# Dilated attention in steps of four units: scores, values and transposes of two pairs at every fourth step

## What is computed

```python
DIL_PAIRS = ((128, 1), (512, 4), (2048, 16))      # window, dilation

def dilated_attention(q, k, v):                   # per block of 128 queries
    ...
    for gi in range(g):                           # three groups
        sc = einsum('bqhd,bqjhd->bhqj', q_blk[:, :, gi], k_sel) * scale
        sc = where(valid, sc, NEG_INF)
        m = max(sc); e = exp(sc - m); z = sum(e)
        o = einsum('bhqj,bqjhd->bqhd', e / z, v_sel)
        outs.append(o); lses.append(m + log(z))
    wgt = softmax(stack(lses))
    out = sum(wgt * stack(outs))
```

## Time and profile before

| | |
|---|---|
| median of 3 runs | 1209.13 us (1208.7 to 1209.37) |
| the profiled execution's own time | 1208.3 us |
| its span | 1206.5 us |
| PE busy in it | 1194.9 us, 99% |
| DVE busy | 840.1 us, 70% |
| ACT busy | 648.6 us, 54% |
| POOL busy | 219.7 us, 18% |
| granted TensorE clock, mean | 0.999 |

### The profile page before, as it was taken

The page is one execution under the profiler, slowest core; times in us unless marked ns, Lnnn a source line. Parts: engine busy times, 40 slices in busy tenths (PEclk is TensorE's granted clock), DMA queues, the critical chain, the costliest instruction groups (busy, mean ns, idle before and its releaser), DMA issues.

```text
span 1206.5 us, 18986 instructions
## 1 busy us (share of the span) xinstructions
PE 1194.9 (99%) x7681; PEld 1047.4 (87%) x7681; DVE 840.1 (70%) x1207; ACT 648.6 (54%) x887; POOL 219.7 (18%) x160
## 2 busy tenths in 40 slices
PE   9999999999999999999999999999999999999998
PEld 9988898888898888889888888898878899888886
DVE  7878768754467856886979754487875576676863
ACT  5575465543455556455555534456576545555452
POOL 2500010000011211331310000010010795545100
PEclk9999999999999999999999999999999999999999
DMA  9723456555548665664355565654544455556551
GB/s 254 250 87 124 140 175 187 197 181 203 179 147 272 199 203 160 186 207 156 114 183 186 177 207 176 209 174 156 179 171 140 171 183 184 178 179 196 184 190 55
DMA packets 162071, 214.08 MB, mean 177 GB/s; under 512 B 5260, under 2 KB 117199, under 8 KB 161983
## 3 DMA queue, kind: packets, MB, share of 16 engines
q1 hardware_dynamic: 161182, 211.41, 54.3%
q10 hardware_dynamic: 608, 0.99, 0.3%
q0 software_dynamic: 192, 0.46, 0.2%
HBM read 205.50 MB, written 1.05 MB: 171 GB/s over the span
## 4 chain that ended last, share of the span: by engine, by line
PE 92%; DVE 3%; ACT 2%; issue 1%; DMA 1%; SPq 0%; DVEq 0%; ACTq 0%
PE ps L541 45%; PE ps L556 20%; PE ps L561 11%; PE ps L641 4%; PE ps L742 3%; PE ps L779 2%; PE ps L750 2%; PE ps L583 2%; DVE wlo L1618 1%; ACT whi L1156 1%; PE ps L607 1%; DVE XT L1756 1%; DMA raw<-in_od_w_in_dram 1%; PE ps L867 1%; PE ps L1031 0%
## 5 line engine op out<-in xcount | busy, mean ns | idle before, releaser
L1618 DVE TENSOR_TENSOR wlo<-raw,whi 128x2048 fp32r<-128x2048 f32 (+1 forms) x167 | 383.8, 2300 | 143.3 <-ACT whi L1156 143.0
L1156 ACT ACTIVATE whi<-raw 128x2048 fp32r<-128x2048 f32 x188 | 357.8, 1906 | 170.3 <-PE ps L541 131.4
L556 PE MATMUL ps<-XHL,whi 128*128 128x512 f32 x1152 | 287.8, 394 | 0.0
L556 PEld LDWEIGHTS ps<-XHL,whi 128*128 128x128 f32 x1152 | 207.8, 189 | 38.1
L561 PEld LDWEIGHTS ps<-XHL,wlo 128*128 128x128 f32 x1152 | 154.8, 190 | 11.6 <-DVE wlo L1618 1.6
L561 PE MATMUL ps<-XHL,wlo 128*128 128x256 f32 x1152 | 158.5, 282 | 0.3 <-DVE wlo L1618 0.3
L541 PE MATMUL ps<-whi,XHL 128*128 128x512 f32 (+1 forms) x576 | 145.2, 345 | 0.0
L2360 POOL TENSOR_TENSOR wlo<-raw,whi 128x512 fp32r<-128x512 f32 x88 | 119.3, 1388 | 141.4 <-ACT whi L1156 141.1
L541 PE MATMUL ps<-whi,HL 128*128 128x512 f32 (+1 forms) x416 | 144.8, 373 | 0.0
L541 PE MATMUL ps<-whi,HH 128*128 128x512 f32 x384 | 143.3, 390 | 0.0
L541 PE MATMUL ps<-wlo,HH 128*128 128x512 f32 x368 | 139.4, 389 | 0.0
(11 more groups left out here) (273 smaller groups left out, 1738.9 us busy)
## 6 DMA issues: line engine op xcount, KB each, us to landing
raw<-in_mlp_w_dram SPq DMA_DIRECT2D x64, 1024.0 KB, 5.3
raw<-in_od_w_in_dram SPq DMA_DIRECT2D x36, 1024.0 KB, 5.3
raw<-in_w_in_dram SPq DMA_DIRECT2D x24, 1024.0 KB, 5.1
raw<-in_w_ffn_gate_dram SPq DMA_DIRECT2D x12, 1024.0 KB, 5.2
raw<-in_w_ffn_up_dram SPq DMA_DIRECT2D x12, 1024.0 KB, 5.2
raw<-in_w_ffn_down_dram SPq DMA_DIRECT2D x12, 1024.0 KB, 5.0
TB<-TA SPq DMA_DIRECT2D x96, 64.0 KB, 2.0
raw<-in_w_branch_dram SPq DMA_DIRECT2D x6, 1024.0 KB, 5.0
```

What stands on the lines that cost most here:

```text
L556: pe.matmul(b[m][:, :], w[m][c][0], XHL[:, c, :], start=c == 0, stop=False)
L1156: act.activation(whi_of(n), raw_of(n), ACT.Copy, scale=1.0).then_inc(*tell(s_whi, ("whi", n)))
L1618: dve.tensor_tensor(wlo_of(n), raw_of(n), f32(whi_of(n)), ALU.subtract).then_inc(*tell(s_wlo, ("wlo", n)))
```

## The change

The first 24 units go four at a time. At every fourth step PE has the scores of four units, then the values of two pairs, then the transposes of four units; the three steps between have only their slabs. DVE takes the four maxima at that step and two softmaxes at each of the two steps behind it; ACT takes the four exponentials. The two pairs' values share a bank, and their outputs become one operation of 256 columns on ACT and one on DVE. SN and PT (3 x 512 columns) are cut into four buffers of 384 for these units, the statistics get a fourth row. The last eight units go as before, with the values of pairs 10 and 11 together at step 26. Cut to its core:

```diff
+FOURS = 24
+
+def dilated_scores(s):
+    if s < FOURS:
+        return range(s, s + 4) if s % 4 == 0 else ()
+    return (s, s + 1) if s < 32 and s % 2 == 0 else ()
+
+def dilated_begun(s):
+    if s < FOURS:
+        return dilated_scores(s)
+    return (s,) if s < 32 else ()
+
+def dilated_scaled(s):
+    if s <= FOURS:
+        return {1: (s - 1, s), 2: (s, s + 1)}.get(s % 4, ())
+    return (s - 1,) if s < 33 else ()
+
+def dilated_turns(s):
+    if s <= FOURS:
+        return range(s - 4, s) if s and s % 4 == 0 else ()
+    return (s - 2,) if FOURS + 2 <= s < 34 else ()
+
+def dilated_values(s):
+    if 8 <= s <= FOURS and s % 4 == 0 or s == FOURS + 2:
+        g = (s - 8) // 2 if s <= FOURS else FOURS // 2 - 2
+        return (g, g + 1)
+    return ((s - 4) // 2,) if FOURS + 4 <= s < 35 and s % 2 == 0 else ()
+
+def before(u):
+    first, k = (EVEN, 3) if u < ODD else (ODD, 4) if u < LAST else (LAST, 3)
+    return u - k if u - k >= first else first - 1
...
+        def unit_of(t, u):
+            if kind_of(u)[0] != DIL:
+                return t[:, u % 3, :]
+            return t[:, :, :].rearrange("p a n -> p (a n)")[:, 384 * (u % 4):384 * (u % 4) + 384]
...
-            def values(g):
-                b = bank(("value", g))
+            def values(*gs):
+                b = bank(("value", gs[0]))
...
+            def attend_dilated(s):                                    # PE
+                for u in dilated_scores(s)[::2]:
+                    scores(group_of(ODD + u))
+                gs = [ODD // 2 + g for g in dilated_values(s)]
+                if gs:
+                    values(*gs)
+                for u in dilated_turns(s):
+                    transposes(ODD + u)
...
-                attend(ODD, 32, s)
+                attend_dilated(s)
...
-                if u >= 3:
-                    once.wait_ge(*at(("turned", u - 3)))
+                if before(u) >= 0:
+                    once.wait_ge(*at(("turned", before(u))))
...
+            def attend_dilated(s):                                    # ACT
+                gs = [ODD // 2 + g for g in dilated_values(s)]
+                if len(gs) == 2:
+                    outputs(*gs)
+                for u in dilated_turns(s) if s <= FOURS else ():
+                    if act_turns(ODD + u):
+                        probs(ODD + u)
+                for u in dilated_begun(s):
+                    exponentials(ODD + u)
+                for u in dilated_turns(s) if s > FOURS else ():
+                    if act_turns(ODD + u):
+                        probs(ODD + u)
+                if len(gs) == 1:
+                    outputs(*gs)
...
+            def attend_dilated(s, beside):                            # DVE
+                for u in dilated_begun(s):
+                    maxima(ODD + u)
+                for u in dilated_scaled(s):
+                    softmax(ODD + u)
+                for u in dilated_turns(s):
+                    if not act_turns(ODD + u):
+                        probs(ODD + u)
+                beside()
+                if dilated_values(s):
+                    outputs(*(ODD // 2 + g for g in dilated_values(s)))
...
-                attend(ODD, 32, s, lambda: added_pieces(s - 1))
+                attend_dilated(s, lambda: added_pieces(s - 1))
```

More of the change, by code:

```diff
@@ L766, in value_parts @@
                 return [(v[:, kt, w * n:w * n + w], (kt * S, kt * S + S), (0, S), kt == 0, kt == 1) for kt in range(2)]
[L768 to L780 removed]
+            def values(*gs):
+                b = bank(("value", gs[0]))
+                for g in gs:
+                    for u in members(g):
+                        once.wait_ge(*at(("probs", u)))
+                        for event in values_ready(u):
+                            once.wait_ge(*at(event))
+                    parts = {u: value_parts(u) for u in members(g)}
+                    for k in range(len(parts[members(g)[0]])):
+                        for u in members(g):
+                            v, (lo, hi), (a, z), start, stop = parts[u][k]
+                            p0, n, _, _ = place_of(u)
+                            m = pe.matmul(b[p0:p0 + n, a:z], v, unit_of(PT, u)[:, lo:hi], start=start, stop=stop)
+                    m.then_inc(*tell(s_value, ("valued", g)))
+            def attend_dilated(s):
[6 more added lines that the diff above has]
+                    transposes(ODD + u)
             def attend(first, n, s):
@@ L1227, in probs, with outputs @@
                 once.wait_ge(*at(("turned", u)))
-                if u >= 3:
-                    once.wait_ge(*at(("valued", group_of(u - 3))))
-                act.activation(PT[:, u % 3, 0:w], ps[bank_of.get(("turn", u), 0)][:, 0:w], ACT.Copy, scale=1.0).then_inc(
+                if before(u) >= 0:
+                    once.wait_ge(*at(("valued", group_of(before(u)))))
+                act.activation(unit_of(PT, u)[:, 0:w], ps[bank_of.get(("turn", u), 0)][:, 0:w], ACT.Copy, scale=1.0).then_inc(
                     *tell(s_act_out, ("probs", u), ("taken", "turn", u)))
-            def outputs(g):
-                _, _, c, (t0, t1) = place_of(members(g)[0])
-                h, v = OH[:, c, t0:t1], ps[bank_of.get(("value", g), 0)][:, 0:t1 - t0]
-                if g < 4:
-                    h, v = h.rearrange("p (r c) -> p r c", c=64), turned(v)
-                once.wait_ge(*at(("valued", g)))
-                act.activation(h, v, ACT.Copy, scale=1.0).then_inc(*tell(s_xhi, ("ohi", g)))
+            def outputs(*gs):
+                _, _, c, (t0, _) = place_of(members(gs[0])[0])
+                _, _, _, (_, t1) = place_of(members(gs[-1])[0])
+                h, v = OH[:, c, t0:t1], ps[bank_of.get(("value", gs[0]), 0)][:, t0:t1]
+                if gs[0] < 4:
+                    h, v = h.rearrange("p (r c) -> p r c", c=64), turned(v)
+                once.wait_ge(*at(("valued", gs[-1])))
+                act.activation(h, v, ACT.Copy, scale=1.0).then_inc(*tell(s_xhi, *[("ohi", g) for g in gs]))
+            def attend_dilated(s):
[12 more added lines that the diff above has]
+                    outputs(*gs)
             def attend(first, n, s):
@@ L1678, in maxima @@
                 kind, _ = kind_of(u)
-                b = ps[bank_of.get(("score", u), 0)]
+                b, st = ps[bank_of.get(("score", u), 0)], stat_of(u)
                 once.wait_ge(*at(("scored", u)))
-                if u >= 3:
-                    once.wait_ge(*at(("turned", u - 3)))
-                    once.wait_ge(*at(("soft", u - 3)))
+                if before(u) >= 0:
+                    once.wait_ge(*at(("turned", before(u))))
+                    once.wait_ge(*at(("soft", before(u))))
                 if kind in (NA, DIL, MOBA):
@@ L1729, in attend @@
                     softmax(u)
-                if not paired and 0 <= s - 2 < n and not act_turns(first + s - 2):
-                    probs(first + s - 2)
                 if beside is not None:
```

53 lines of the change are left out of this document (29 added, 24 removed).

## The result

The changed kernel takes 1211.61 us, the median of 14 runs (1210.41 to 1213.15), against 1208.80 for the kernel before on the same chip (14 runs): ratio 1.0022, 95% interval 1.0015 to 1.0029. It is slower by 2.8 us, where 0.4 faster was forecast; the range held the time. The profiled execution took 1211.98 us. In the changed kernel scores are line 796, values 836, transposes 804, pieces and value slabs 595, the other slabs 610 and 615, maxima 1770, the additions of pieces 1849.

What follows compares the result with a forecast made beforehand. PE was taken to bound the kernel, with DVE as close after step 24. Terms -3.2 + 4 x 0.4 + 0.4 + 2.2 - 1.2 = -0.2, taken as -0.4, gave 1208.7 us; range 1204.9 to 1212.2.

Steps and rivals of the forecast that it cites:

- merging: PE's scores, values, transposes and returns to slabs: fewer switches of kind save 0.53 us per four units, 3.2 us in all.
- ninth bank, steps 4 to 20: Merged steps need nine banks of eight, so PE waits for DVE's maxima: 0.4 us at each of five steps.
- step 24, the waits: Fourth transposes and next piece wait for banks until DVE's additions, queued behind unit 24's maxima: 2.2 us, between 1.3 and 2.4.
- probs in the tail: With PE later against DVE and ACT, its three waits for ACT's probs after step 24 go: 1.2 us back.
- Rival (b): DVE, held by POOL's sines, reaches blocks late; 0.8 us late at five blocks adds 4.0 us: 1212.7 us, chance 0.16.
- Rival (c): PE pays the switch of kind per bank, so the 3.2 us saving fails: 1211.9 us, chance 0.05.
- rival (a): Banks are read in time and never hold PE: 1204.7 us; chance 0.24 including a half-way case.
- A loss in low halves or loads would refute my account of what is covered: Sign against the claim that DVE's low halves and SP's loads have enough slack off the path to cost nothing.

Runs made afterwards that it cites:

- transposes first: Changed kernel with PE doing transposes, values, scores up to step 24, probs taken first, step 24's additions ahead of the maxima: 1206.52 us, ratio 0.9987 to the kernel before.
- additions first: Changed kernel with DVE adding step 23's two pieces before the maxima of unit 24 at step 24: 1208.62 us, ratio 1.0001 to the kernel before.
- eight writes: Changed kernel with eight idle one-column DVE writes added at the start: 1210.90 us, ratio 1.0015 to the kernel before.
- fillers: Changed kernel with PE multiplying ones into unused bank columns in both step 24 waits; with five and three: 1209.07 us, again 1210.04 us.
- seven writes: Changed kernel with seven idle one-column DVE writes added at the start: 1210.78 us, ratio 1.0015 to the kernel before.
- a single write: Kernel with all units in pairs and buffers of four, plus one idle DVE write at the start: 1209.70 us, ratio 1.0011 to the kernel before.

## Why the prediction was wrong

**The sum.** From the rows of the runs, for the stage of the changed kernel:

| term | forecast | measured | from |
|---|---|---|---|
| merging | -3.2 | -2.6 | the stage with transposes first, -2.51, with 0.08 more waits for probs |
| ninth bank, steps 4 to 20 | +2.0 | +1.75 | additions first: -1.76, less the -2.6 and 0.9 fewer waits for probs |
| step 24, the waits | +2.2 | +2.25 | scores to scores, 8.89 us with eight writes, 6.64 with the additions first |
| step 24, the clock | none | +1.5 | 10.36 instead of 8.89 us |
| probs in the tail | -1.2 | -0.7 | 1.21 us before, 0.53 left |
| stage | -0.2 | +2.2 | in the trace 224.53 - 222.27 = 2.26 |
| outside the stage | none | +1.2 | 295.45 - 294.24 |

The table is of the profiled execution, in which the clock fell. With the 0.6 us that the clock costs on the average, the terms give 2.5, beside the 2.8 that the medians show.

**What was right.** The kind and the place of the waits, but for step 4. The fourth transposes of step 24 start 1.15 us after a wait for the first additions, the piece 0.62 us after one for the second, together as long as forecast to 0.1 us. The transposes of steps 8, 16 and 20 are 0.38 us longer than with transposes first (1.78 against 1.40), for a forecast of 0.4; step 12 has 0.55, step 4 none where 0.4 was taken. Rival (b) happened in one block of the changed kernel, and in small. At step 12 DVE is still adding the sines when the first transposes end, as (b) has it, and its maxima begin 0.85 us after the start of these transposes (485.79 us) instead of 0.68 at steps 8, 16 and 20 (DVE in order of time):

```profile
486.04 0.69 DVE L2082 TENSOR_TENSOR BIG<-BIG,TB 128x512 f32<-128x512 f32 x1 [1.48 <-POOL TB L2519]
486.64 0.55 DVE L1770 CUSTOM_DVE_ANT_0 SN<-ps,BIG 128x384 f32<-128x384 f32 x1
```

That is the 0.17 us that step 12 has beyond the 0.38 of the others. At steps 8, 20 and 24 DVE stood idle ahead of its maxima (4.7, 1.3 and 4.9 us). The sum recorded for (b) has the scaling end at 2.83; by its own 0.55 us behind POOL that is 2.72, which leaves DVE 0.1 us of slack. Rival (c) did not happen: two pairs of scores take 1.49 us instead of 1.64 in two. The rule on rotating banks (the Trainium skill, "Perfetto Trace Analysis", section Matmuls) did not give the time of rival (a): the rotation hid the reads only where the reader was not itself queued behind PE.

**The step that failed** in the stage is "At step 24 ... I take 2.2 us", carried into the sum as if a wait cost its length and nothing else. PE was idle twice within 2.3 us there, and in three of the four profiles of this order the clock that was granted behind it was half, for 3.41 us in the first of them, which costs 1.5 us. The kernel before has waits up to 0.8 us with no fall behind them, so its rows did not show it; the prediction could have asked what PE is granted behind its longest idle time. With full fillers the clock stayed at 1.0 in all three profiles. One profile with the waits idle stayed at 1.0 as well, so the profiles alone don't settle the cause; the mean clocks of all executions, 0.9984 with the waits idle and 0.9989 with fillers, point the same way.

**Two terms were mis-sized.** Merging saves 0.43 us per four units, not 0.53. Scores and values give 0.15 each (1.64 to 1.49), for 0.17 and 0.16 forecast; the rest is in the transposes and the returns, where the slab's first eight matmuls take 2.05 us behind a block (transposes first) instead of 1.85. And the tail gave back 0.7 of 1.2 us: at step 32 ACT's probs stand behind exponentials that wait 1.5 us for DVE's maxima, so a later PE does not remove that wait. These two terms alone turn the sign of the forecast: the kernel with fillers has neither the half clock nor the late product, and its stage is 0.7 us longer than before, where 0.2 less was forecast.

**One loss had no place in the method.** The 1.2 us behind the third attention hang on DVE's instruction count, and by the medians they are the largest term that the sum lacked. The prediction asked who is late for whom within the stage, and put everything outside it at nothing without a reason. Its own sign, "A loss in low halves or loads would refute my account of what is covered", did show, but not by the path that it had in mind: the low half that PE waits for is made some 500 us behind the stage.

By medians the loss is 2.8 us, not the profiles' 3.5. A clock that falls in some executions only, as the means on record have it, would make about that difference.

## What to carry to other kernels

A wait of the engine that bounds the kernel can have a price beyond its length: look at the granted clock behind the longest idle times, and where a change would make such a wait, ask what the engine that is waited for could do later instead. Merging the work of a step pays (here 2.6 us) only if each bank's reader does not itself wait for the merged work; turning the order so that the readers come before the new writes kept nearly all of it and made the fastest kernel of this study, 0.9987 of the time before. Where an unchanged part far away gets longer, compare it instruction by instruction before explaining it with the change: an edit can move it by the mere number of instructions.

## What the runs showed of the hardware

- The same two idle times of PE (1.15 and 0.62 us) were followed by a granted clock of 0.5 in three profiles (two of the changed kernel, one with seven writes) and of 1.0 in a fourth (eight writes). A wait of 2.81 us came with 6.83 us at 0.5, from 0.7 us before the wait's end. The Trainium skill ("TensorE: Matmul & The Clock Gate", Part 1) says that the monitor's look at the engine runs free of the program, so that the same kernel comes out differently from run to run. The four profiles fit that, and so does the mean clock of 0.9984 over 47 executions, which lies between that of the kernel before (0.9990) and one lower by a fall in each (0.0014); no kernel here was profiled both with the fall and without it.
- DVE makes a pause of about 0.3 us, with nothing waited for, that stays at its place in the count of its instructions: with eight instructions more ahead of it the late product was record 1601 instead of 1473, and a single write made it so in another kernel. What the pause is was not found out. In all six profiles that show it, a packet of 8192 bytes on an instruction queue (q14) starts 1.7 to 1.8 us after the start of the late addition, which speaks for the supply of instructions and does not show it. Where the pause let a DVE product meet the change of POOL's products, 0.87 us became 1.82, and the program lost 1.2 us.
- A DVE product of two SBUF tiles that starts while a POOL product runs ends 0.55 us behind that one: so in nine products of these traces, which took from 0.72 to 1.83 us by how much of POOL's was left (0.17 to 1.28 us).
- A matmul of ones by ones, 128 columns in 32-bit floats, is two records and takes 0.22 us (24 records in 2.68 us, up to the start of the transposes behind them).
